# Final normalisation of a hybrid decoder step: the sample rows summed on TensorE, two roots in place of three, the root applied on ScalarE for three row sets

## The reference

```python
x = x + f            # f: the two chosen experts' rows, each times its combine weight
y = xf * lax.rsqrt(jnp.mean(xf * xf, axis=-1, keepdims=True) + RMS_EPS) * norm_final_w
```

## Time and profile before

| what | value |
|---|---|
| runs | 1179.15, 1181.93 and 1182.7 us, median 1181.93 |
| profiled execution | 1178.33 us, its span 1176.2 us |
| PE busy over the span | 1077.2 us (92%) |
| DVE, ACT, POOL busy | 486.1, 288.4, 211.5 us |
| memory traffic over the span | 162 GB/s |
| last scatter landed, sample rows' load issued | 1147.88 us |
| last compute instruction | starts 1170.85 us |
| last store issued | 1172.15 us |

### The profile page before, as it was taken

One profiled execution on the slowest core, in us unless ns is written; L12 is line 12 of the kernel. 1 busy time (PEld: TensorE's weight loads), 2 busy tenths in 40 slices (PEclk: granted clock), 3 DMA queues, 4 the chain that ended last, 5 costly groups with the idle time before them and its releaser, 6 DMA issues. The chain is left out here.

```text
span 1176.2 us, 25289 instructions
## 1 busy us (share of the span) xinstructions
PE 1077.2 (92%) x10717; PEld 827.6 (70%) x10717; DVE 486.1 (41%) x1152; ACT 288.4 (25%) x585; POOL 211.5 (18%) x269
## 2 busy tenths in 40 slices
PE   5999999799999999999999999999995999986874
PEld 5888888688888887888777888886453555543541
DVE  4455555565565635555456201001454422211126
ACT  3243224345544441000254110000111211111102
POOL 4001000144553500000000058000001222212120
PEclk9999999899999999999999999999996999999997
DMA  8032222020000003229312222900977899999975
GB/s 243 1 104 65 56 56 57 23 56 4 4 4 4 4 13 103 59 72 234 95 37 72 68 76 55 269 35 23 408 286 276 336 416 415 414 417 416 417 316 218
DMA packets 114049, 183.08 MB, mean 156 GB/s; under 512 B 10369, under 2 KB 88733, under 8 KB 105242
## 3 DMA queue, kind: packets, MB, share of 16 engines
q1 hardware_dynamic: 107293, 168.59, 41.2%
q0 software_dynamic: 5168, 8.56, 2.0%
q10 hardware_dynamic: 1485, 4.39, 1.0%
HBM read 173.24 MB, written 17.55 MB: 162 GB/s over the span
## 5 line engine op out<-in xcount | busy, mean ns | idle before, releaser
L192 PE MATMUL rk_ps<-xT,rk_w 128*128 128x260 f32 x768 | 172.6, 385 | 0.0
L192 PEld LDWEIGHTS rk_ps<-xT,rk_w 128*128 128x128 f32 x768 | 144.6, 190 | 26.9 <-issue 2.7
L192 PE MATMUL psv<-xT,w_merge 128*128 128x260 f32 x480 | 107.7, 383 | 0.0
L192 PEld LDWEIGHTS psv<-xT,w_merge 128*128 128x128 f32 x480 | 91.1, 190 | 13.9
L2141 DVE SCALAR_TENSOR_TENSOR ex_sg<-tl_psA,ex_slot_rs,ex_sg 128x128 f32<-128x128 f32 x32 | 11.2, 351 | 139.7 <-ACT ex_sg L1941 139.5
L1414 POOL TENSOR_TENSOR spare<-spare,sv 128x4096 f32<-128x4096 f32 x1 | 8.9, 8855 | 277.6 <-DVE r_all L1383 277.6
L192 PE MATMUL uv_psu<-xT,w_uv 128*128 128x260 f32 x256 | 57.5, 383 | 1.2 <-ACTq L1084 1.2
L192 PE MATMUL mg_psp<-ya,w_merge 128*128 128x260 f32 x256 | 57.6, 383 | 0.0
L192 PE MATMUL psv<-xT,w_uv 128*128 128x260 f32 x256 | 57.4, 382 | 0.0
L192 PE MATMUL mg_psp<-r_all,w_merge 128*128 128x260 f32 x256 | 57.4, 382 | 0.0
L192 PEld LDWEIGHTS uv_psu<-xT,w_uv 128*128 128x128 f32 x256 | 48.0, 190 | 8.8 <-ACTq L1084 1.7
(11 more groups left out here) (497 smaller groups left out, 2007.2 us busy)
## 6 DMA issues: line engine op xcount, KB each, us to landing
wd<-in_moe_w_down SPq DMA_DIRECT2D x15, 1024.0 KB
rk_w<-in_w_in SPq DMA_DIRECT2D x24, 512.0 KB, 6.2
tl_x<-in_moe_w_down SPq DMA_DIRECT2D x9, 1024.0 KB, 20.3
w_uv<-in_w_in SPq DMA_DIRECT2D x16, 512.0 KB, 5.4
w_merge<-in_w_in SPq DMA_DIRECT2D x16, 512.0 KB, 4.3
xT<-in_moe_w_gate SPq DMA_DIRECT2D x5, 1024.0 KB, 20.1
xT<-in_moe_w_up SPq DMA_DIRECT2D x5, 1024.0 KB, 23.6
bonus_all<-in_moe_w_gate SPq DMA_DIRECT2D x5, 1024.0 KB, 19.8
```

Of the source, the lines that this page charges most:

```text
L192: last = eng.matmul(out[:, h, 0:TH], weights[:, k, :], xT[:, k, h * TH:(h + 1) * TH], start=(k == 0), stop=(k == NK - 1))
```

## The change

The sample rows' sum moves to TensorE: two more 8x8 diagonals are built (`diag_s`), and six float32 matmuls of 512 columns each put `x + w0*y0 + w1*y1` into `psC[0:8]`, in TensorE's queue ahead of `combined(psA, 0)` and `combined(psT, 2)`. ScalarE squares the sample rows from there. On VectorE the sample's sum and its own root are gone; there are two roots, over the columns of sample, tile 0 and tile 1, and over those of tiles 2 and 3. For the sample and tiles 0 and 2, VectorE now multiplies the sum in PSUM by the gain into SBUF (`gained`), before the root is known, and ScalarE multiplies the row by its root afterwards (`scaled_act`, a Copy with a scale per row). Each `gained` waits for the square of the same banks. Tiles 1 and 3 are handled as before. The stores keep their order; three of them now wait for ScalarE.

```diff
@@ names and semaphores
+        diag_s = w_hi[0:TS, 4 * P:4 * P + 2 * TS].rearrange("p (c s) -> p c s", c=2)
+        s_fps, s_fm, s_fo_act, s_froot = (sem("f_" + n) for n in ("ps", "m", "o_act", "root"))
@@ SyncE: stores of the results
-            for i, j in enumerate(final):
-                eng.wait_ge(s_fo, i + 1)
-                if j < NT:
-                    eng.dma_start(a["y_prompt"][0, j * P:(j + 1) * P, :], fx[:, j, :]).then_inc(s_out, 16)
-                else:
-                    eng.dma_start(a["y_sample"][:, 0, :], fxs).then_inc(s_out, 16)
+            eng.wait_ge(s_fo_act, 1)
+            eng.dma_start(a["y_sample"][:, 0, :], fxs).then_inc(s_out, 16)
+            for j, (done, n) in ((0, (s_fo_act, 2)), (1, (s_fo, 1)), (2, (s_fo_act, 3)), (3, (s_fo, 2))):
+                eng.wait_ge(done, n)
+                eng.dma_start(a["y_prompt"][0, j * P:(j + 1) * P, :], fx[:, j, :]).then_inc(s_out, 16)
@@ TensorE: between kept(psT, 2) and combined(psA, 0)
+            eng.wait_ge(s_fy[NT], 16)
+            for h in range(2):
+                at_h = slice(h * 512, (h + 1) * 512)
+                eng.matmul(psC[0:TS, h, :], m.ident[0:TS, 0:TS], fxs[:, at_h], start=True, stop=False, skip_group_check=True)
+                for c in range(2):
+                    last = eng.matmul(psC[0:TS, h, :], diag_s[:, c, :], fys[0:TS, c, at_h], start=False, stop=(c == 1),
+                                      skip_group_check=True)
+            last.then_inc(s_fps, 1)
@@ ScalarE: final stage
+            def scaled_act(i, dst):
+                n = size[final[i]]
+                eng.activation(dst, dst, ACT.Copy, scale=rstd[0:n, i:i + 1]).then_inc(s_fo_act, 1)
-            eng.wait_ge(s_fs, 1)
-            square_final(0, fxs, TS)
+            eng.wait_ge(s_fps, 1)
+            square_final(0, flat(psC[0:TS, :, :]), TS)
             eng.wait_ge(s_fp, 1)
             square_final(1, flat(psA[:, :, :]), P)
-            eng.wait_ge(s_fs, 2)
+            eng.wait_ge(s_fs, 1)
             eng.wait_ge(s_fsq, 1)
             square_final(2, fx[:, 1, :], P)
...
             square_final(3, flat(psT[:, :, :]), P)
-            eng.wait_ge(s_fs, 3)
+            eng.wait_ge(s_froot, 1)
+            eng.wait_ge(s_fm, 2)
+            scaled_act(0, fxs)
+            scaled_act(1, fx[:, 0, :])
+            eng.wait_ge(s_fs, 2)
             eng.wait_ge(s_fsq, 3)
             square_final(4, fx[:, 3, :], P)
+            eng.wait_ge(s_froot, 2)
+            eng.wait_ge(s_fm, 3)
+            scaled_act(3, fx[:, 2, :])
@@ VectorE: behind the diagonals, before s_diag
+            for c in range(2):
+                step.did(eng.tensor_scalar(diag_s[:, c, :], m.ident[0:TS, 0:TS], m.weight[0:TS, c, at[NT]:at[NT] + 1], None, ALU.mult))
@@ VectorE: final stage
-            sum_up(NT)
-            root(0, 1)
+            def gained(src, dst, gain):
+                eng.tensor_tensor(dst, src, gain, ALU.mult).then_inc(s_fm, 1)
+
+            eng.wait_ge(s_fps, 1)
+            eng.wait_ge(s_fsq, 1)
+            gained(psC[0:TS, :, :], by_half(fxs), by_half(gf[0:TS, :]))
             sum_up(1)
-            scaled(0, fxs, fxs, gf[0:TS, :])
-            root(1, 3)
+            eng.wait_ge(s_fp, 1)
+            eng.wait_ge(s_fsq, 2)
+            gained(psA[:, :, :], by_half(fx[:, 0, :]), by_half(gf[:, :]))
+            root(0, 3)
+            eng.sem_inc(s_froot, 1)
             sum_up(3)
-            scaled(1, psA[:, :, :], by_half(fx[:, 0, :]), by_half(gf[:, :]))
+            eng.wait_ge(s_fp, 2)
+            eng.wait_ge(s_fsq, 4)
+            gained(psT[:, :, :], by_half(fx[:, 2, :]), by_half(gf[:, :]))
             scaled(2, fx[:, 1, :], fx[:, 1, :], gf[:, :])
             root(3, 5)
-            scaled(3, psT[:, :, :], by_half(fx[:, 2, :]), by_half(gf[:, :]))
+            eng.sem_inc(s_froot, 1)
             scaled(4, fx[:, 3, :], fx[:, 3, :], gf[:, :])
```

## The result

The changed kernel is slower. Its median is 1184.28 us over 10 runs, against 1178.64 over 10 of the kernel before; the ratio of the undisturbed runs is **1.0041, 95% interval [1.0027, 1.0055]**, that is 4.8 us (3.2 to 6.5). The forecast was 3.0 us.

What follows compares the result with a forecast made beforehand. VectorE's chain to tile 2's store bounds the final stage: sample's sum at 1157.42 plus 15.34 ends the second root at 1172.76, issue at 1173.97, 3.0 us later. Median 1181.93 becomes 1184.9 us, range 1180.8 to 1190.0.

Steps and rivals of the forecast that it cites:

- What bounds the stage: Final stage: after the last scatter and expert-row loads, VectorE is the path; its 5 us less work stood at the front.
- The sample's sum on TensorE: Six matmuls behind tile 2's x part: 5.4 us plus 0.2 for the diagonals, sum there at 1157.42 us.
- The chain behind it: From the sample's sum through squares, gains, sums and two roots: 15.34 us; tile 2's store issued 3.0 us later than before.
- The clock rival: Sample's 8x8 matmuls on TensorE don't hold the clock: 5.1 us more, 1190.0 us, or 1193.8 if later sums slow; chance 0.15.
- My evidence against: Against a falling clock: 66 TensorE records at 827.3 to 830.9 us, nearly all 8 columns but 128 rows, ran at 1.00.
- the line of 0.3%: Whole time: smallest change a measurement can tell, about 3.5 us, which put the line to slower at 1185.5 us.
- the side that had 0.37: Whole time: the outcome slower, beyond 1185.5 us, given chance 0.37, against 0.58 for same and 0.05 for faster.
- TensorE sooner: x parts at full clock end 1.7 us sooner, sample's rows bind: 1183.6 us; lower bound 1181.5; chance 0.15.
- only tile 3's issue: Last stores: the end hangs on tile 3's issue alone and moves 2.2 us, to 1184.1; counted within the forecast's own range.
- the first rival: The one called TensorE sooner: x parts at full clock end early, then the sample's expert rows bind; chance 0.15.
- The median: Whole time: 3.0 us added to the earlier median of 1181.93 gives 1184.9 us, 0.25% more.

Runs made afterwards that it cites:

- point 1: Changed kernel with the sample's six matmuls on 128x128, on 128 rows and 8 columns, or 8 rows and 128 columns: stages 31.60, 31.68, 33.42 us against 33.11.
- point 4: Kernel before, tile 2's store cut to half its rows, then half its columns: span's end 4.75, then 3.91 us after tile 3's issue, against 4.05.
- point 6: Changed kernel with the sample's sum back on VectorE and each root's last instruction raising ScalarE's semaphore: stage 29.68 us, ratio 0.9989 to the kernel before.

## Why the prediction was right, and where not

*What bounds the stage: right.* From the last scatter the chain ran on VectorE, and what VectorE had less to do at the front bought nothing (28.38 us without the first root, against 28.32).

*The sample's sum on TensorE: right.* Forecast 9.54 us after the stage's start (5.4 us of matmuls and 0.2 for the diagonals), measured 1160.11 - 1150.59 = 9.52. Its 5.4 us were taken over from matmuls of 128 rows and 128 columns of weights; the six took 5.3 us with 8x8 as with 128x128 (point 1). The prediction writes two speeds of TensorE as 1.2 and 2.4 GHz. No run shows the clock in GHz; what the windows show is a granted clock of 0.52 and 0.99.

*The chain behind it: right, but for terms of 0.3.* With the clock held (128x128), the first root started 15.70 us into the stage, forecast 15.69. Not forecast were the semaphore instructions behind the roots, which the prediction put at nothing. The first cost 0.17 us; the second stood beside ScalarE's way and cost next to none, so that tile 2's issue came at 26.26, forecast 26.09. From there to the end it was 5.34 us and not 5.24, another 0.1. The stage came to 31.60 where 28.32 + 3.0 = 31.3 was said.

*The clock rival: the clock fell, but not at its place nor for its price.* I gave 0.15 to a clock that falls within the sample's matmuls, at 8 to 12 us. In the changed kernel it fell when they had ended, and hit tile 0's sum: 1.5 us of stage, where the rival's price was 5.1. In the two other kernels with 8 rows it did fall within them, but only for the last records. I had tile 0's square ready 0.12 us before VectorE wanted it and named no rival for that thin cover; nearly all of the missing time came in there. TensorE was busy without a gap from 1148.64 to 1168.87, and the clock fell all the same. My evidence against, matmuls of 8 columns at 1.00, was evidence on columns, and by point 1 it is the rows that go with the fall.

*The sum:* 3.0 forecast, + 0.2 for the semaphore instruction, + 0.1 behind tile 2's issue, + 1.5 for the clock, is 4.8, as measured. That took the ratio across the line of 0.3%, to the side that had 0.37. The clock's share was in no term of the forecast, and its size is partly chance: with the sum alone on TensorE, where the clock fell sooner, the stage was 1.8 us above the 32.7 expected without a fall.

*TensorE sooner, and only tile 3's issue: neither.* In the changed kernel's profile the x parts ran mostly at half clock (0.56 from 1149.6 to 1152.5), as forecast; in the kernel with 8 rows and 128 columns they ran at 1.00 (1151.8 to 1155.3), ended early, and TensorE waited 0.18 us for the sample's rows, which is the first rival's mechanism. That code is the same in both kernels, and in both TensorE had waited 2.20 us for the gather before it, so this looks like a draw between executions; the later fall took its gain away there. As to the stores, for the changed kernel the two transfers decide, as forecast; for the kernel before they hardly do (point 4).

*The median.* 1184.9 was forecast from a median of 1181.93 over three runs, and 1184.28 came with the median of before at 1178.64. The closeness is partly chance; the difference was 4.8 and not 3.0.

## What to carry to other kernels

Work that is taken off the busiest engine of a stage saves nothing where it stood in that engine's wait for data: the first root, 2.2 us of VectorE, left a wait of 0.83 us when it was gone, and the stage was 28.38 us against 28.32. Before moving the first item of a chain, ask when it is ready on the new engine and what stands behind it in that queue: here the sample's sum was ready 9.5 us into the stage and not 5.2 and pushed tile 0 back with it. And look at the granted clock behind small matmuls, not only within them: with 8 rows fed (8x8) it was 0.50 in most of tile 0's sum, which took 5.40 us; with 128 rows fed it was 1.00 there and the sum took 3.60 and 3.70, while the sample's own matmuls took 5.3 us either way. That is one profile each.

## What the runs showed of the hardware

- The granted clock of TensorE fell from 1.00 to 0.50 in three kernels that had about 5 us of matmuls with 8 rows fed, whether with 8 or 128 columns. In two of them the engine had been busy without a gap since the transposes; in the third it had one gap of 0.18 us before these matmuls. The clock held in three kernels with 128 rows, with 8 or 128 columns. One profile each. A float32 matmul of 512 columns took 0.86 us from start to start in each case at 1.00 (1154.80 to 1155.66 in the changed kernel).
- After a wait of 3.88 us TensorE's next 3.3 us ran at a granted clock of 0.51 (point 6); in the kernel before, after 1.98 us, it ran at 1.00 (1154.0 to 1157.6) and tile 0's sum took 3.70 us.
- The same code at the same place ran at 1.00 in one execution and 0.72 in another (6.9 and 9.6 us for 16 records). Much of the scatter between the runs of one kernel may come from such draws; that was not tested.
- Beside a GpSimd multiply of 128x1024 in SBUF (2.34 us) a VectorE instruction of three elements per partition took 2.31 us, and 0.17 without it; beside VectorE's sum of tile 3 both took longer (4.58 for 2.60, 3.35 for 2.34).
- ScalarE's row with a scale per partition took 1.15 us, as forecast from the 0.09 us between two shorter rows.
- A semaphore instruction behind a wait cost VectorE 0.17 us; with the increment on the root's last instruction the next row started 0.20 us after that instruction's start, with the separate one 0.33.
- Storing 64 partitions of 1024 values did not shorten the pair of transfers: 4.75 us from tile 3's issue to the span's end for 4.05, at 123 to 303 GB/s. Why was not tested.
